# Matmuls that nothing reads, added to the recurrence and to the search for the best tokens

## The reference

```python
def _gla_scan(q, k, log_f, v, s0):            # the recurrence, chunk by chunk, 6 heads of 64 channels
    def step(s, xs):
        a = jnp.cumsum(gc, axis=2)
        decay = jnp.exp(jnp.where(causal[:, :, None], a[:, :, :, None, :] - a[:, :, None, :, :], -jnp.inf))
        scores = jnp.sum(qc[:, :, :, None, :] * kc[:, :, None, :, :] * decay, axis=-1)
        o = jnp.einsum('bhts,bhsv->bhtv', scores, vc) + jnp.einsum('bhtk,bhkv->bhtv', qc * jnp.exp(a), s)
        s_new = jnp.exp(a_last[:, :, 0, :, None]) * s + jnp.einsum('bhsk,bhsv->bhkv', kc * jnp.exp(a_last - a), vc)

def _expert_choice_ffn(h, w_router, w_gate, w_up, w_down):
    cap = EC_CAPACITY_FACTOR * t // N_EXPERTS                     # 64 latent tokens, 32 context tokens
    vals, idx = lax.top_k(softmax(h @ w_router).T, cap)
    out = (silu(h[idx] @ w_gate) * (h[idx] @ w_up)) @ w_down * vals   # added back at idx
```

## Time and profile before

| | before |
|---|---|
| median of 3 runs | 4014.54 us (4014.53 to 4024.01) |
| the profiled execution | 4021.41 us, its span 4019.6 us |
| PE busy | 3707.4 us, 92% of the span |
| VectorE busy | 2356.4 us, 59% |
| ScalarE busy | 1757.2 us, 44% |
| mean granted clock of TensorE | 0.939 |

### The profile page before, as it was taken

How to read it: one execution, slowest core, us unless ns; L and a number is a source line. 1 busy time by engine, 2 the same in 40 slices (tenths; PEclk the granted TensorE clock), 3 DMA queues, 4 the chain that set the end, 5 groups by cost and what they waited for, 6 DMA issues and landing times.

```text
span 4019.6 us, 52277 instructions
## 1 busy us (share of the span) xinstructions
PE 3707.4 (92%) x19680; PEld 2875.3 (72%) x19680; DVE 2356.4 (59%) x3495; ACT 1757.2 (44%) x2858; POOL 314.6 (8%) x411
## 2 busy tenths in 40 slices
PE   8997997998999587998999998999999999889998
PEld 7885576666788364556887776788777878657877
DVE  7865836886964957886773327566333332564332
ACT  3336635886333745885222327322233222453222
POOL 0110010100111000001210000111000000000001
PEclk9998597999999588999999999999999999999999
DMA  7562025995654026994883320477223223302222
GB/s 273 178 179 66 2 74 182 354 350 212 230 194 116 1 74 231 365 360 171 278 265 125 104 84 1 138 233 231 100 83 128 95 90 104 141 27 89 95 94 74
DMA packets 167009, 622.29 MB, mean 155 GB/s; under 512 B 19661, under 2 KB 21238, under 8 KB 165630
## 3 DMA queue, kind: packets, MB, share of 16 engines
q1 hardware_dynamic: 118384, 433.15, 30.9%
q0 software_dynamic: 44160, 158.10, 12.5%
q10 hardware_dynamic: 4238, 27.90, 1.8%
HBM read 598.30 MB, written 17.88 MB: 153 GB/s over the span
## 4 chain that ended last, share of the span: by engine, by line
PE 84%; DVE 7%; ACT 5%; DMA 2%; issue 2%; SPq 0%; ACTq 0%; POOL 0%; DVEq 0%; POOLq 0%; PEldq 0%
PE psum L2278 23%; PE psum L2291 12%; PE psum L846 12%; PE psum L2046 8%; PE psum L933 5%; PE psum L1000 4%; PE psum L2065 4%; PE psum L775 3%; PE psum L1231 1%; PE psum L1241 1%; DMA ring<-wtile 1%; PE psum L783 1%; PE psum L2002 1%; PE psum L1518 1%; PE psum L1528 1%
## 5 line engine op out<-in xcount | busy, mean ns | idle before, releaser
L799 ACT CAST small_r<-ring 128x1024 fp32r<-128x1024 f32 x264 | 276.1, 1048 | 1079.8 <-PE psum L846 336.0
L803 DVE TENSOR_TENSOR ring_r<-ring,small_r 128x1024 fp32r<-128x1024 f32 x264 | 322.8, 1225 | 689.6 <-ACT small_r L799 689.3
L799 ACT CAST PB_r<-ring 128x1024 fp32r<-128x1024 f32 x344 | 357.6, 1050 | 566.0 <-PE psum L2278 327.3
L803 DVE TENSOR_TENSOR ring_r<-ring,PB_r 128x1024 fp32r<-128x1024 f32 x344 | 414.1, 1221 | 267.4 <-ACT PB_r L799 265.9
L2278 PE MATMUL psum<-H_r,ring_r 128*128 128x512 f32 x1344 | 335.3, 392 | 0.0
L2278 PE MATMUL psum<-H_r,small_r 128*128 128x512 f32 x1344 | 327.7, 396 | 0.0
L2278 PE MATMUL psum<-H_r,PB_r 128*128 128x512 f32 x1344 | 318.3, 389 | 0.0
L2278 PEld LDWEIGHTS psum<-H_r,small_r 128*128 128x128 f32 x1344 | 253.4, 189 | 60.5
L2278 PEld LDWEIGHTS psum<-H_r,ring_r 128*128 128x128 f32 x1344 | 252.4, 188 | 55.0
L2278 PEld LDWEIGHTS psum<-H_r,PB_r 128*128 128x128 f32 x1344 | 252.4, 188 | 53.1
L846 PE MATMUL psum<-H_r,small_r 128*128 128x512 f32 (+1 forms) x1040 | 275.5, 368 | 0.1
(11 more groups left out here) (414 smaller groups left out, 6851.8 us busy)
## 6 DMA issues: line engine op xcount, KB each, us to landing
ring<-wtile SPq DMA_DIRECT2D x800, 512.0 KB, 5.1
spare<-wmod POOLq DMA_DIRECT2D x97, 512.0 KB, 4.9
H<-wmod POOLq DMA_DIRECT2D x48, 512.0 KB, 4.5
PB<-wmod POOLq DMA_DIRECT2D x48, 512.0 KB, 4.2
X<-wmod POOLq DMA_DIRECT2D x47, 512.0 KB, 5.0
h_rows<-PB POOLq DMA_DIRECT2D x10, 512.0 KB, 3.6
PB<-wmod SPq DMA_DIRECT2D x4, 1024.0 KB, 15.3
PB<-wshift SPq DMA_DIRECT2D x4, 1024.0 KB, 17.4
```

Source lines behind the costliest of these rows:

```text
L799: nc.scalar.copy(high(j), slot(g0 + j)).then_inc(high_ready.sem, 1)
L803: nc.vector.tensor_tensor(low(g0 + j), slot(g0 + j), high(j).bitcast(F32), ALU.subtract).then_inc(low_ready.sem, 1)
```

## The change

`keep_clock(out, n)` issues `n` matmuls of the identity (128x128) with as many columns of the constants as `out` has. Nothing reads their output. They are f32, like the other matmuls of these stages, and each is its own accumulation.

In the recurrence, three of them on 256 columns stand in `scores` of every wanted unit, behind the waits and ahead of the scores. They write the free half of the first bank of the unit's pair. That makes 36 x 3 in layer 0 and 24 x 3 in layer 1. In the search, VectorE's `max_index` raises a new semaphore `round_taken` in each round, and TensorE, behind its last token rows and ahead of the wait for `pick_ready`, waits for each of the eight increments and issues two fillers on 384 columns: 16 in each layer.

```diff
+            b_rt = round_taken.reserve(CAP_LAT // 8)
+        def keep_clock(out, n):
+            for _ in range(n):
+                nc.tensor.matmul(out, ident, con[:, 0:out.shape[1]], start=True, stop=True)
...
                         if d and x - nw // 2 in (0, 1):
                             eng.wait_ge(between_cleared.sem, b_cl + x - nw // 2 + 1)
+                        keep_clock(bank[2 * (x % 2)][:, 2 * P:4 * P], 3)
                         t0 = ch * P
...
                 for u in range(2, n_tok):
                     token_rows(u)
+                for r in range(CAP_LAT // 8):
+                    eng.wait_ge(round_taken.sem, b_rt + r + 1)
+                    keep_clock(bank[0][:, 0:384], 2)
                 eng.wait_ge(pick_ready.sem, b_pk + 1)
...
                     V(eng, nc.vector.max(best, work))
-                    nc.vector.max_index(where[:, 8 * r:8 * r + 8], best, work)
+                    nc.vector.max_index(where[:, 8 * r:8 * r + 8], best, work).then_inc(round_taken.sem, 1)
                     V(eng, nc.vector.match_replace(work, best, work, -1.0))
```

More of the change, by code:

```diff
@@ L293, in build @@
         lam_ready = sig("lam_ready")
+        round_taken = sig("round_taken")
         values_saved, values_spread = sig("values_saved"), sig("values_spread")
```

## The result

The changed kernel is slower: its time stands to that of the kernel before as 1.0063, with a 95% interval of 1.0045 to 1.008. The medians of six runs each are 4047.74 and 4023.94 us, a difference of 23.8 us; the forecast was +26.

What follows compares the result with a forecast made beforehand. TensorE carries 84% of the chain, at half clock in the recurrences, where VectorE is 97% full in layer 0 and the bound in layer 1. 14 + 11 + 1 = +26 us on 4014.54: predicted 4041, range from around the low ends (4022) to 4078.

Steps and rivals of the forecast that it cites:

- The unit and the block: Recurrence, layer 0: a unit at full clock with its block of three fillers takes 2.19 + 1.47 = 3.66 us.
- The clock: Recurrence: the granted clock rises from half within one or two units of each start and should stay up in layer 0.
- The prediction's test (L1585): Head sums in the trace before, same shape as fillers: after the one at 512.39 us the clock rose to 1.00.
- Layer 0: Recurrence of layer 0, 36 wanted units with 108 fillers: about +14 us (6 to 23).
- The starts: Start of layer 0 and of its cell 1: nothing hides blocks there, some at half clock; together +10.3 us.
- cells 1 to 4: Layer 0: +1.3 us each, +5.2, with -1.5 for head sums; layer 1: half the cells late, 4 x 1.5 = +6.
- cell 5: Layer 0: 22.6 us before and after, so no change, since its second half has full clock already.
- Layer 1: Recurrence of layer 1, 24 wanted units with 72 fillers: +11 us (3 to 22).
- The search: Both searches, 32 fillers: +0.5 us per layer for late fillers; taken +1 for both layers (-4 to +8).
- A block is nearly free: Rival: fillers run in gaps that the records count as busy, leaving only the gain; about -18, 3997 us; chance 0.14.
- The clock isn't raised: Rival: the clock stays at half and the fillers cost their full time; +160, 4175 us; chance 0.04.
- the clock that comes and goes: Rival: the clock falls at each TensorE wait, each cell's first two blocks run at 2.87 us; 4070 us; chance 0.14.

Runs made afterwards that it cites:

- e3: The changed kernel with one filler instead of three in each wanted unit, search fillers kept; ratio to the kernel before 1.0096 (1.0078 to 1.0114).
- e5: The changed kernel with two fillers instead of three in each wanted unit, search fillers kept; ratio to the kernel before 1.0068 (1.0046 to 1.0089).
- e1: The changed kernel with the recurrence's fillers alone, those of the search taken out; ratio to the kernel before 1.0059 (1.0042 to 1.0076).
- e9_bridge: The changed kernel without recurrence fillers, with the search's and eight more of 384 columns behind the turned indices; ratio to the kernel before 0.9992 (0.9977 to 1.0007).
- e6_kick: The changed kernel with three fillers only in each cell's first wanted unit, none in the search; ratio to the kernel before 1.0048 (1.0031 to 1.0065).

## Why the prediction was right, step by step

**The unit and the block.** Forecast 2.19 + 1.47 = 3.66 us, measured 3.68 with a block of 1.50. A cell was forecast at 20.9 us and takes 21.0 (from first scores within blocks to those of the next; 19.4 before by this count, where the prediction has 19.6). The price came from L1585, the same shape in the trace of before. At the low end of 1.28 us a block would have cost less than the 1.35 us that full clock gives back per unit, and the cells that TensorE bounds would have grown by 0.2 us in place of 1.3. The estimate of about 430 ns a filler from the Trainium skill ("FP8 and Floating Point Precision", on true FP32, with the gap of "TensorE: Matmul & The Clock Gate") would give 1.29 us for a block; no row here has one that short at full clock.

**The clock.** It rose in layer 0 as forecast, first from 394 us on, right behind the first block; it fell in each of TensorE's two long waits ahead of the second piece and of cell 1, and held from 435 us on. e3 and e5 show how near it was: one filler didn't raise it ahead of the head sums, two raised it in one place only after 56 us. The prediction's test (L1585) didn't settle how many are needed, only that three would be likely.

**Layer 0**: forecast +14, measured +16.4. The starts up to the first scores of cell 1 cost 9.9 us (10.3 forecast, with 1.4 of it for the block behind them), cells 1 to 4 cost 4.9 (3.7), cell 5 costs 1.6 (0). The nothing for cell 5 came from a misread start. In the kernel before, the stretch from 498.72 us, with no transposed keys in it, is the last unit of cell 4; the first unit of cell 5 starts behind the head sum, at 502.59, and has them again:

```profile
503.34 0.47 PE L1524 MATMUL psum<-con,PB 128*128 128x128 f32 x1
```

So cell 5 took 18.8 us up to TensorE's idle, and not 22.6. In the changed kernel it takes 22.8 us from its first block (518.76) to the idle (541.59), close to the 22.6 forecast for it but 4.1 more than before; 1.5 of them vanish in the last wait, which shrinks from 2.22 to 0.74 us.

**Layer 1**: forecast +11, measured +17.2. The first block is 2.9 us as forecast. The term that was sized too small is the one of cells 1 to 4 and the last stretch. The prediction took 1.5 us for each of four cells (some 3 us in half of them) and +2 at the end; from first wanted scores to first wanted scores the five stretches grew by 4.7, 3.7, 0.3, 2.3 and 0.1 us, 11.1 in sum where it had 6, and the last by 3.2. The clock fell in TensorE's wait ahead of each of cells 1 to 4, and not of half of them, and in three cells it took two blocks to raise it. How much of this one execution is chance e1 tells, with the same recurrence and 152.4 us, and untouched code, with 139.0 to 144.8: the cost of the fillers in layer 1 is between 8 and 17 us.

**The search**: forecast +0.5 per layer for the late fillers, measured 0.5 and 0.5. That the clock would fall in the wait for the rows was taken, and it did.

**What wasn't forecast**: behind the recurrence of layer 1 the stage up to the router took 52.8 us instead of 55.3, the clock being up when it starts; in layer 0 it gained 0.6.

**The sum is nearer than its parts.** In the profiled executions the two recurrences cost 33.6 us where 25 was forecast, and the searches 1.0; the stages behind the recurrences gave 3.1 back, which wasn't forecast. That makes +31.5, but the spans differ by only 27.8 us: the rest of the kernel, which is the same code in both, was some 4 us shorter. In e1 the recurrences cost 29.8, and the median of e1 is 26.6 above that of the kernel before. The signs and the mechanism are the forecast ones; that 26 met 23.8 so closely is in part luck.

**The rivals.** "A block is nearly free" falls: 1.50 us against its point of 1.35. "The clock isn't raised" would have been right for one filler a unit, or for fillers of a quarter of the array, these near the price given (4162.4 us, 4175 forecast). The one of the clock that comes and goes is half true: in layer 1 of the profiled execution the first block of the first five cells ran at half clock, wholly or in part, and the second block too in three of them.

## What to carry to other kernels

A filler in a list where the engine has no idle time costs its full duration (with one filler at half clock the unit went from 3.54 to 4.69 us, by the filler's 1.15), and full clock gives back only the difference between the unit at both clocks: work out both from rows of the trace, and ask first whether another engine is as full, since then even a free clock brings nothing. Fillers belong in TensorE's waits, where they have to end before the wait does (in e9_bridge they ran 0.5 us over), and not ahead of the first work for which another engine waits. Where a stage's time depends on when the clock happens to rise, the same code gives several times, so look at more than one trace before a gain of some microseconds is believed.

## What the runs showed of the hardware

- A TensorE busy 60.00 of 60 us can stand at 0.50 of its clock all the while, with most of its matmuls on tiles of half or a quarter of the array. With three 128x128 fillers a unit it rose, with three of 64x64 of nearly the same duration it didn't (units of 3.68 and 6.09 us; the latter in one execution).
- The rise under one and the same pattern of work came 12 us behind a cell's first block in two cells of layer 1 and after 56 us in layer 0 (e5_two), and the fall without fillers came after 3 to 14 us of units without any (e6_kick).
- In the kernel before the clock fell in the slice from 524 us, behind an idle time of TensorE of 2.22 us.
- Untouched code of the recurrence took 143.1 to 147.4 us in layer 0 and 139.0 to 144.8 in layer 1, by when its own head sums raised the clock. The expert stage of layer 0, the same code behind its first matmuls, took 302 to 318 us. The kernel before lies between 4006.2 and 4038.2 us over all its executions; how much of that comes from these stages is not shown.
